# A two-block fp32 sequence model on one core: the norm sum of a head's second half placed one projection piece later, and the first loads dealt out to the queues in another way

## The reference

```python
h = rms_norm(x, g_pre)
proj = jnp.einsum('bsd,de->bse', h, w_in)
q_h, f_h, i_h, z_h, q_a, k_a, v_a, z_a = jnp.split(proj, SPLIT_POINTS, axis=-1)
o_h = hgrn2(q_h, f_h, i_h, lb)      # 8 heads of 128: S_t = diag(f_t) S_{t-1} + (1 - f_t) i_t^T, o_t = S_t^T q_t
o_h = rms_norm(o_h, g_head).reshape(B, S, HG_WIDTH).astype(z_h.dtype) * jax.nn.silu(z_h)
...                                 # sliding window attention on q_a, k_a, v_a, gated by z_a
y = jnp.einsum('bse,ed->bsd', jnp.concatenate([o_h, o_a], axis=-1), w_out)
return x + rms_norm(y, g_post)
```

## Time and profile before

| | us |
|---|---|
| median of three runs | 3549.38 |
| the three runs | 3542.32 to 3551.21 |
| the profiled execution, its own time | 3538.84 |
| its span, first to last instruction | 3537.0 |

### The profile page before, as it was taken

One profiled execution on the slowest core, in us unless ns is written; L12 is line 12 of the kernel. 1 busy time (PEld: TensorE's weight loads), 2 busy tenths in 40 slices (PEclk: granted clock), 3 DMA queues, 4 the chain that ended last, 5 costly groups with the idle time before them and its releaser, 6 DMA issues.

```text
span 3537.0 us, 59949 instructions
## 1 busy us (share of the span) xinstructions
PE 3351.6 (95%) x18080; PEld 2723.0 (77%) x18080; DVE 2059.3 (58%) x5230; ACT 1568.5 (44%) x3221; POOL 1456.2 (41%) x1830
## 2 busy tenths in 40 slices
PE   8999999999999999999999999989998999899988
PEld 6888887666777888887666779977886799778866
DVE  5766665767256766665767254257665332576653
ACT  5545443444245545443444243145554331456542
POOL 6555564332624555564332621123344221333352
PEclk9999999999999999999999999999999999999999
DMA  5111112111321111112111322211112521111124
GB/s 151 37 31 36 30 36 58 45 37 31 101 90 51 37 31 36 30 36 57 46 37 31 101 90 72 67 45 28 46 53 65 162 76 60 41 40 32 53 82 147
DMA packets 217951, 206.47 MB, mean 58 GB/s; under 512 B 17949, under 2 KB 185261, under 8 KB 216669
## 3 DMA queue, kind: packets, MB, share of 16 engines
q1 hardware_dynamic: 197536, 137.80, 13.9%
q0 software_dynamic: 12208, 47.03, 3.8%
q10 hardware_dynamic: 7920, 18.19, 1.6%
HBM read 148.04 MB, written 37.01 MB: 52 GB/s over the span
## 4 chain that ended last, share of the span: by engine, by line
PE 71%; DVE 11%; issue 7%; ACT 4%; POOL 2%; DMA 2%; DVEq 1%; ACTq 0%; SPq 0%; POOLq 0%
PE banks L1024 24%; PE banks L1309 7%; PE banks L1193 5%; PE banks L1245 5%; PE banks L1217 4%; PE banks L1331 4%; PE banks L1396 3%; PE banks L1139 2%; PE banks L1149 2%; PE banks L1272 2%; PE banks L1161 2%; PE banks L1387 2%; PE banks L1062 1%; DVE BB L2112 1%; DVE SM L2264 1%
## 5 line engine op out<-in xcount | busy, mean ns | idle before, releaser
L1024 PE MATMUL banks<-H,whi 128*128 128x512 f32 x3200 | 1044.7, 408 | 4.9 <-ACT VT L1536 3.9
L1024 PEld LDWEIGHTS banks<-H,whi 128*128 128x128 f32 x3200 | 572.2, 188 | 183.8 <-issue 65.6
L1024 PE MATMUL banks<-H,wlo 128*128 128x512 f32 x1600 | 631.2, 395 | 0.0
L677 POOL CAST whi<-raw 128x1024 fp32r<-128x1024 f32 x150 | 165.0, 1100 | 924.4 <-PE banks L1024 383.1
L680 POOL TENSOR_TENSOR wlo<-raw,whi 128x256 fp32r<-128x256 f32 (+1 forms) x246 | 402.1, 1651 | 12.1
L1309 PE MATMUL banks<-H,whi 128*128 128x346 f32 (+1 forms) x1536 | 381.0, 331 | 10.0 <-DVEq L431 8.1
L1024 PEld LDWEIGHTS banks<-H,wlo 128*128 128x128 f32 x1600 | 301.3, 188 | 69.1
L2426 DVE TENSOR_SCALAR_CACHE_REDUCE SP<-banks 128x346 f32<-128x346 f32 (+3 forms) x432 | 201.1, 513 | 220.4 <-PE banks L1374 219.6
L1309 PEld LDWEIGHTS banks<-H,whi 128*128 128x128 f32 x1536 | 272.1, 193 | 17.2 <-issue 14.0
L1678 ACT ACTIVATE SM<-SM,stt 128x256 f32<-128x256 f32 (+1 forms) x256 | 124.7, 488 | 320.9 <-DVE stt L2269 320.9
L1309 PE MATMUL banks<-H,wlo 128*128 128x346 f32 (+1 forms) x768 | 250.7, 326 | 0.0
(11 more groups left out here) (311 smaller groups left out, 7291.0 us busy)
## 6 DMA issues: line engine op xcount, KB each, us to landing
raw<-in_w_in SPq DMA_DIRECT2D x148, 512.0 KB, 3.9
raw<-in_w_out SPq DMA_DIRECT2D x64, 256.0 KB, 2.6
XT<-x_resident POOLq DMA_DIRECT2D x18, 512.0 KB, 4.1
x_resident<-XT POOLq DMA_DIRECT2D x18, 512.0 KB, 2.9
raw<-in_w_out SPq DMA_DIRECT2D x18, 512.0 KB, 4.6
RQ<-QR SPq DMA_DIRECT2D x112, 64.0 KB, 2.0
XB<-x_resident POOLq DMA_DIRECT2D x14, 512.0 KB, 4.6
SR<-cat_resident SPq DMA_DIRECT2D x16, 448.0 KB, 3.6
```

The lines of the kernel that those rows point to most:

```text
L677: link(nc.gpsimd.tensor_copy(hi, src))
L1024: last = nc.tensor.matmul(bank(half if bk is None else bk), w[:, slot, k, :], H[:, part, a:a + 512], start=k == 0 and n == 0, stop=k == DT ...
```

## The change

Two independent parts.

In the recurrent heads the norm of the second half of the previous head moves within the head that follows. On PE `head_sum(hh - 1, 1)` stands behind the projection piece of slot 0. On ACT `norm_rstd(hh - 1, 1)` goes from slot 0 to slot 2, behind the decays. On DVE `normed(hh - 1, h - 1, 1)` goes from slot 0 to slot 2, behind `carry` and ahead of `cumulate`.

At the start `gall` goes from SP to ACT's queue behind tiles 1 and 3, tiles 4 to 7 go from ACT to POOL's queue ahead of the splits, and `lbp` is issued by ACT behind the first root.

```diff
@@ sync
-            with nc.allow_non_contiguous_dma(reason="a few short parameter vectors"):
-                sp.dma_start(gall[:, 0:DEPTH, :], g_pre.rearrange("l (t p) -> p l t", p=P)).then_inc(g("par_in"), 16)
@@ gpsimd
+            for s in range(4, ST):
+                pool.dma_start(XS[:, s, :], x[0, s * P:s * P + P, :]).then_inc(g(f"xt_in{s}"), 16)
             for e in range(2):
                 split_in(0, e, None)
@@ tensor, head
                         nc.tensor.transpose(psum[3][:, 2 * P:3 * P], IT[:, par, cs], ident).then_inc(g("sd_ready"), 1)
-                        if c == 0 and not first:
-                            head_sum(hh - 1, 1)
                         if nxt:
                             project(h * 4 + 4 + c // 2, (c // 2) % 2, h * 8 + 8 + c, c2)
                         else:
                             last_project(c)
+                        if c == 0 and not first:
+                            head_sum(hh - 1, 1)
@@ scalar
-            for s in (1, 3, 4, 5, 6, 7):
+            for s in (1, 3):
                 act.dma_start(XS[:, s, :], x[0, s * P:s * P + P, :]).then_inc(g(f"xt_in{s}"), 16)
             with nc.allow_non_contiguous_dma(reason="a few short parameter vectors"):
-                act.dma_start(lbp[:, :, :], lb_param.rearrange("l (t p) -> p l t", p=P)).then_inc(g("lb_in"), 16)
+                act.dma_start(gall[:, 0:DEPTH, :], g_pre.rearrange("l (t p) -> p l t", p=P)).then_inc(g("par_in"), 16)
...
             root_in(0)
+            with nc.allow_non_contiguous_dma(reason="a few short parameter vectors"):
+                act.dma_start(lbp[:, :, :], lb_param.rearrange("l (t p) -> p l t", p=P)).then_inc(g("lb_in"), 16)
             square_in(half)
@@ scalar, head
-                        if c == 0 and not first:
-                            norm_rstd(hh - 1, 1)
                         if c == 2 and nxt:
                             head_log(h + 1, 1 - par)
...
                             decays(hh * 4 + c // 2 + 2, 1 - par, c // 2 - 2)
+                        if c == 2 and not first:
+                            norm_rstd(hh - 1, 1)
```

## The result

The changed kernel takes 3582.6 us (median of 4 runs, 3568.79 to 3587.63), the kernel before 3548.3 beside it. The ratio is 1.0092, with a 95% interval of 1.0066 to 1.0119: it is slower by 34 us, where 9.6 was forecast and 3567 was the upper end of the range. The profiled execution after has a span of 3567.0 us, 30.0 more than before.

A forecast was written before the change was run, and what follows sets the result against it. PE, busy 95% of the span, was taken to bound the kernel. Heads +7.8 us (24.5 lost, 16.7 gained) plus start +1.8 gave +9.6 on 3549.38: 3559.0 us, range 3552 to 3567.

The forecast's parts named there:

- Slot 0, PE: Heads 1 to 7, both layers: moving the sum behind the piece removes PE's wait for the squares and its restart, gaining 16.7 us.
- ACT: Inverse root in slot 2 of the heads: costs nothing, done 0.7 us before DVE asks for it.
- DVE, slot 2: Heads 1 to 6: the two products delay `AT`, so PE waits 2.62 us in slot 3; 12 x 2.04 = 24.5 us lost.
- Head 7: Last head, without `cumulate`: the two products in slot 2 cost nothing, bounds 0 and 2 x 2.04 us.
- the whole of it becomes PE's wait: Slot 3 of heads 1 to 6: no slack hides DVE's 2.04 us, so PE's wait grows from 0.58 to 2.62 us.
- Rival 3: Slot 2: POOL slows DVE's gate multiplication from 0.69 to 2.60 us, 23 us more, total 3582; chance 0.06.
- Start: Up to PE's first projection matmul: `gall` lands 2.7 us later, 0.9 of it slack, so +1.8 us.
- the price of the weights beside `gall`: Start: 1920 weight packets take turns with `gall`'s packets and cost it 3.5 us.
- Rival 1: Heads as forecast, but `gall` lands early and the start gains 1.2 us, total 3556; chance 0.2.
- The even counts: Start: SP's and ACT's queues passed 421 packets each from 8 to 12 us, read as queues advancing one packet against one.
- Rival 4: Start: ACT is held by its own issue of `lbp` until `gall` is in, 2.4 us more, total 3561.4; chance 0.12.
- Rival 2: Slot 2: the two products vanish as in slot 0, so the 16.7 us gain stands alone, total 3534.5; chance 0.07.

The follow-up runs named there:

- e8: Kernel before with the sum behind slot 0's piece, ACT's root behind slot 0's decays, DVE's products left in slot 0, old start: 3527.9 us, 0.49% faster than before.
- e1: Kernel before with the head part of the change alone, the start as before: as slow as the whole change.
- e3: e1 with three unread 128x512 matmuls added on PE ahead of slot 3's wait for `AT`: 34 us faster than e1 by the medians, 29 by the ratios.
- e5: Kernel before with the sum behind slot 0's piece, ACT's root behind slot 0's decays, DVE's products in slot 1, old start: 3536.9 us.
- e2: Kernel before with the start part of the change alone, the heads as before: time cannot be told from the kernel before.
- e4: Kernel before with only DVE's two products moved from slot 0 to slot 2, sum and root still in slot 0: 3593.1 us.
- e6: e1 with one unread 128x512 matmul added on PE ahead of slot 3's wait for `AT`: 3566.1 us.

## Why the prediction was wrong, point by point

- **Slot 0, PE: right.** -16.7 forecast, -16.5 measured, and e8 has it alone: -17.2 by the medians.
- **ACT: right.** The root in slot 2 was in time; e8 shows that it is so in slot 0 as well, but for 0.65 us of DVE's slack.
- **DVE, slot 2: right in place and size.** 12 waits of 2.7 to 3.0 us, all in slot 3; +25.2 for 24.5. Head 7 cost 0.9, within its bounds of 0 and 4.1.
- **The step that failed** is "the whole of it becomes PE's wait", which I took to be all that it costs. Behind a wait of 2.7 to 3.0 us in work that is otherwise without a pause, TensorE was granted half its clock, and the following piece ran 1.6 to 3.0 us longer: 16.5 us by the profile of the changed kernel, 28.2 by that of e1. e3 takes this away with work that is thrown away, and the heads are back in the forecast's bounds. In the sum it was a missing term as large as the others.
- **It could be read before.** The trace of the kernel before has the same thing outside the heads. PE's timeline and the windows there, in the attention of the first layer:

```profile
862.70 0.44 PE L1149 MATMUL banks<-cst,SM 128*128 128x128 f32 x2 [1.94 <-DVE SM L2264]
...
863.88 1.22 PE L1024 MATMUL banks<-H,whi 128*128 128x512 f32 x2
```

```profile
862.00:864.00 2.00, 1.30 (x7) 0.62 (x7) 2.00 (x5) 0.18 (x1) 1.61 (x2) 0.87 0.01 5
864.00:866.00 2.00, 2.00 (x7) 1.01 (x7) 1.94 (x7) 1.32 (x7) 0.00 (x0) 0.50 0.00 0
866.00:868.00 2.00, 2.00 (x11) 1.51 (x11) 0.75 (x5) 1.22 (x6) 0.00 (x0) 0.78 0.03 8
```

  A wait of 1.94 us, and behind it the pair of projection matmuls takes 1.22 us, where it takes 0.62 to 0.73 at the full clock. Summed over the trace of before, the granted clock is at half for 110 us, none of it in the heads. One of 1.93 us behind the heads has the full clock behind it (1.00 from 576 to 582), so the length of one wait does not decide alone. A wait nearer in length to the new ones stands later in the same trace, with the half clock behind it:

```profile
576.98 0.73 PE L1024 MATMUL banks<-H,whi 128*128 128x512 f32 x2 [1.93 <-ACT VT L1536]
...
2699.13 1.70 PE L1387 MATMUL banks<-cst,SP 128*16 128x128 f32 x9 [2.75 <-DVE SP L2436]
```

```profile
2699.00:2701.00 2.00, 1.87 (x11) 1.76 (x12) 1.88 (x8) 0.98 (x3) 2.00 (x4) 0.71 0.00 0
2701.00:2703.00 2.00, 1.73 (x7) 1.29 (x6) 1.97 (x5) 2.00 (x4) 1.92 (x3) 0.50 0.00 0
```

  The waits in the heads were up to 1.3 us and none was followed by it; I was about to make 12 waits of 2.6 and had rows of what follows such a wait, and priced them at their length. The Trainium skill, "TensorE: Matmul & The Clock Gate", section "HAM oscillation — how this bites in real kernels", prices such time: what is spent at the half clock, times (1 - 1.2/2.4). The rows agree: from 168 to 174 us of the changed kernel the granted clock is 0.83, 0.50 and 0.82, so (0.17 + 0.50 + 0.18) x 2 = 1.7 us of full-speed work is missing, and the slot is 1.63 longer.
- **Rival 3 gave 3582 and was wrong.** Its mechanism would show as a gate multiplication over 2 us in slot 2; it is 0.69. That its number is that of the result is chance. The same contention was real in slot 1 (e5).
- **Start: right by its sum, half right by its steps.** +1.8 forecast, +1.3 measured (0.8 in e2), and by the times no difference (e2). The new start costs another 0.9 us in slots 5, which the prediction did not have. `gall` was late, by the turns that the weights take. Two things I had not seen: beside the early split on POOL the scalings took 5.61 us instead of 2.74, so that the transposes began 2.75 us later, hidden behind the late `gall`; and the price of the weights beside `gall` is not 3.5 us but some 8, because being late it also meets POOL's large packets. Rival 1 gave the start a gain, with `gall` early; it came at 18.47, so that is refuted. The even counts on which the prediction rejected it do not do so by themselves: two queues that each pass many packets in a turn would also come out even over 4 us, and would hold `gall` up as much. It takes the counts over 0.2 us above to show turns of one packet. Rival 4 did not happen: 0.38 us.
- **Rival 2** (the products vanish) fell as argued. It is true of slot 0, and there the change would have been worth 17 us had it left them.

## What to carry to other kernels

Price a new wait of TensorE by what follows it, too: look in the trace for waits of the same length and read the granted clock behind them, before you set a wait at its own length; where such a wait can't be avoided, matmuls whose result nobody reads can be cheaper than the pause (here by some 30 us over 12 waits). When a step is moved for one engine, move on each other engine only what has to move: here the sum on PE and the root on ACT, and DVE's products already stood where there was room. And a time that fits is not yet a cause: the right number stood beside the wrong rival.

## What the hardware showed that was not expected

- The half clock behind a recurring pause: 8 of the 12 waits of 2.7 to 3.0 us in the changed kernel were followed by it in the profiled execution, 11 of 12 in e1 and in e4, 4 of 12 of 1.8 to 2.2 us in e6, none of those of 1.3 us and below in e3, e5 and e8. In e1 the second layer was hit harder than the first, by the same waits (17.4 and 10.8 us); why, and what picks out the waits that are followed, is open.
- A multiplication over three times as long beside POOL: 0.69 us alone, 2.37 beside a split. And four scalings at 5.61 instead of 2.74 us, though they have one large input only.
- An issue of a DMA of 2048 single values behind another one in ACT's queue took 0.38 us, where SP's issue of a weight tile behind such a one had taken 7.78. What decides this was not tried.
